# Sigmoid products and convolution diagonals on GpSimd, and another order of the taps on VectorE

## The reference

```python
a = _rmsnorm(h, g_pre_mix[l])
u = jnp.einsum("bsd,dc->bsc", a, w_in[l])            # 1024 -> 2560
c_val, c_gate = u[..., :512], u[..., 512:1024]
qkv = u[..., 1024:].reshape(B, S, 3, 8, 64)
glu = c_val * jax.nn.sigmoid(c_gate)
y = depthwise causal convolution of glu, 31 taps, + conv_b
conv_out = silu(layernorm(y))
attn_out = stick-breaking attention of q, k, v (8 heads), normed per head
y = concat([conv_out, attn_out]) @ w_out[l]
```

## Time and profile before

| | before |
|---|---|
| median of 3 runs | 1856.43 us (1854.65 to 1856.76) |
| the profiled execution | 1856.76 us, span 1855.0 us |
| PE busy | 1810.0 us (98%) |
| DVE busy | 953.5 us (51%) |
| ACT busy | 751.0 us (40%) |
| POOL busy | 104.9 us (6%) |
| mean granted clock of PE | 0.987 |

### The profile page before, as it was taken

How to read it: one execution, slowest core, us unless ns; L and a number is a source line. 1 busy time by engine, 2 the same in 40 slices (tenths; PEclk the granted TensorE clock), 3 DMA queues, 4 the chain that set the end, 5 groups by cost and what they waited for, 6 DMA issues and landing times.

```text
span 1855.0 us, 21601 instructions
## 1 busy us (share of the span) xinstructions
PE 1810.0 (98%) x8477; PEld 1482.7 (80%) x8477; DVE 953.5 (51%) x1714; ACT 751.0 (40%) x1475; POOL 104.9 (6%) x151
## 2 busy tenths in 40 slices
PE   8999999999999999999999999999998999999997
PEld 7887888888887777777888888787887788888886
DVE  6666444344334667655344434487984544243345
ACT  7333432323234556645232323333855543233233
POOL 0000010101001111001010101000000000000000
PEclk9999999999999999999999999999997999999999
DMA  7222233333333112112333332232100332333331
GB/s 250 79 70 90 70 113 91 102 91 102 91 102 84 57 46 69 35 57 80 95 99 96 97 98 95 80 93 78 58 1 1 99 106 92 102 91 102 96 97 57
DMA packets 195749, 158.37 MB, mean 85 GB/s; under 512 B 5249, under 2 KB 161153, under 8 KB 195649
## 3 DMA queue, kind: packets, MB, share of 16 engines
q1 hardware_dynamic: 194240, 154.16, 27.0%
q0 software_dynamic: 400, 1.25, 0.3%
q10 hardware_dynamic: 1008, 1.59, 0.2%
HBM read 154.88 MB, written 2.10 MB: 85 GB/s over the span
## 4 chain that ended last, share of the span: by engine, by line
PE 90%; DVE 6%; ACT 3%; issue 1%; DMA 0%; SPq 0%; ACTq 0%; DVEq 0%
PE ps L730 29%; PE ps L731 28%; PE ps L732 28%; PE ps L1158 1%; PE ps L782 1%; DVE sb L1864 0%; DVE sb L1838 0%; PE ps L1046 0%; DVE sb L2394 0%; ACT sb L1379 0%; PE ps L1052 0%; DVE sb L1836 0%; PE ps L841 0%; DMA sb<-in_mem 0%; PE ps L1022 0%
## 5 line engine op out<-in xcount | busy, mean ns | idle before, releaser
L730 PE MATMUL ps<-sb,sb 128*128 128x512 f32 (+3 forms) x2547 | 987.5, 390 | 6.5 <-issue 2.4
L731 PE MATMUL ps<-sb,sb 128*128 128x512 f32 (+3 forms) x2547 | 965.6, 381 | 0.0
L732 PE MATMUL ps<-sb,sb 128*128 128x512 f32 (+3 forms) x2547 | 965.5, 381 | 0.0
L730 PEld LDWEIGHTS ps<-sb,sb 128*128 128x128 f32 (+1 forms) x2547 | 478.3, 189 | 114.2 <-issue 16.2
L732 PEld LDWEIGHTS ps<-sb,sb 128*128 128x128 f32 (+1 forms) x2547 | 478.0, 189 | 92.0
L731 PEld LDWEIGHTS ps<-sb,sb 128*128 128x128 f32 (+1 forms) x2547 | 478.9, 189 | 85.3
L1838 DVE TENSOR_TENSOR sb<-sb,sb 128x512 fp32r<-128x512 f32 x532 | 348.3, 695 | 348.7 <-ACT sb L1360 347.8
L1360 ACT ACTIVATE sb<-sb 128x512 fp32r<-128x512 f32 x532 | 305.8, 622 | 436.5 <-PE ps L732 434.3
L2053 DVE TENSOR_TENSOR sb<-sb,sb 128x512 fp32r<-128x512 f32 x64 | 68.0, 1063 | 177.0 <-ACT sb L1509 177.0
L1519 ACT ACTIVATE sb<-ps 128x512 f32<-128x512 f32 x64 | 38.4, 599 | 208.6 <-PE ps L732 208.6
L658 POOL TENSOR_TENSOR sb<-sb 128x512 f32<-128x512 f32 x64 | 66.9, 1045 | 785.6 <-ACT sb L1519 785.6
(11 more groups left out here) (203 smaller groups left out, 1001.1 us busy)
## 6 DMA issues: line engine op xcount, KB each, us to landing
sb<-in_w_up SPq DMA_DIRECT2D x86, 512.0 KB, 3.9
sb<-in_w_down SPq DMA_DIRECT2D x86, 512.0 KB, 3.9
sb<-in_w_gate SPq DMA_DIRECT2D x22, 512.0 KB, 3.8
sb<-in_a_w_in SPq DMA_DIRECT2D x20, 512.0 KB, 3.7
sb<-in_w_in SPq DMA_DIRECT2D x20, 512.0 KB, 3.6
sb<-in_w_o SPq DMA_DIRECT2D x16, 512.0 KB, 3.9
sb<-in_w_mem_kv SPq DMA_DIRECT2D x8, 512.0 KB, 7.7
sb<-in_w_out SPq DMA_DIRECT2D x8, 512.0 KB, 3.9
```

What stands on the lines that cost most here:

```text
L730: mm(ps, lh, rh, start=start, stop=False, **k)
L731: mm(ps, lh, rl, start=False, stop=False, **k)
L732: return mm(ps, ll, rh, start=False, stop=stop, **k)
```

## The change

The product of the sigmoid with `RB` and the products that make the diagonals go from DVE's queue to POOL's, in the order of the plan, with the same semaphores. The step `dg` goes. In the plan, the taps stand in other numbers and places: ahead of the attention units 5 for each tile behind the first two and 4 for each `v2` slab (66 in all up to `v2_out`, where 45 were, and three behind it), then two behind each `lg`, two more ahead of `bt`, and two at a unit's end. `lo` stands right behind `ev`, `sl` right behind `sp` and `lo`, and `v2_out` behind the last taps of the `v2` slabs.

```diff
--- before.py
+++ after.py
@@ -379,16 +379,10 @@
     TAPS = [(j, k) for j in range(3) for k in range(31)]
     PLAN_C = []
     for n, x in enumerate(IN_FIRST):
-        PLAN_C += [("tile", x), ("w", SL["in", x] + 3), ("ev", x)]
-        if n < 2:
-            PLAN_C += [("lo", x)]
-        else:
-            PLAN_C += [("taps", 2), ("lo", x), ("taps", 1 if x[0] in "qk" else 2)]
+        PLAN_C += [("tile", x), ("w", SL["in", x] + 3), ("ev", x), ("lo", x), ("taps", 5 if n >= 2 else 0)]
     for j in range(4):
-        PLAN_C += [("v2", j), ("w", CH["v2"].first + min(j, 2) + 3)]
-        if j == 3:
-            PLAN_C += [("v2_out",)]
-        PLAN_C += [("taps", 3)]
+        PLAN_C += [("v2", j), ("w", CH["v2"].first + min(j, 2) + 3), ("taps", 4)]
+    PLAN_C += [("v2_out",)]
     BEHIND = [("tile", x) for x in IN_LATER] + [("cv", g) for g in range(3)] + [("ln_sub",)]
     for u in range(8):
         b = BEHIND[u - 1] if u else ("", "")
@@ -399,8 +393,7 @@
         PLAN_C += [("lg", u), ("taps", 2)]
         if u >= 4:
             PLAN_C += [("pt" if u % 2 else "ps", u // 2 - 2)]
-        if BEHIND[u][0] == "cv":
-            PLAN_C += [("dg", u - 4)]
+        PLAN_C += [("taps", 2)]
         if u >= 1:
             PLAN_C += [("bt", u - 1)]
         if u >= 2:
@@ -412,7 +405,7 @@
             PLAN_C += [("lo", b[1])]
         if u >= 4 and u % 2 == 0:
             PLAN_C += [("pr", u // 2 - 2)]
-        PLAN_C += [("taps", 2), ("sl", u)]
+        PLAN_C += [("sl", u)]
         if u >= 1:
             PLAN_C += [("ah", u - 1), ("at", u - 1)]
         if u >= 2:
@@ -422,7 +415,7 @@
             PLAN_C += [("w", CH["v2"].last + min(u, 3) + 4)]
         if u >= 4 and u % 2:
             PLAN_C += [("pl", u // 2 - 2)]
-        PLAN_C += [("taps", 1 if u < 4 else 4 if u < 6 else 100)]
+        PLAN_C += [("taps", 2 if u < 6 else 100)]
     PLAN_C += [("bt", 7), ("ps", 2), ("va", 6), ("ex", 7), ("pr", 2), ("o", (0, 1, 2)), ("ah", 7), ("at", 7), ("kp", 6),
                ("ln_var",), ("pt", 2), ("ln_rs",), ("va", 7), ("kp", 7), ("pl", 2), ("ps", 3), ("pr", 3), ("ln_mul",),
                ("o", (3,)), ("pt", 3), ("silu", 0), ("pl", 3)]
@@ -705,6 +698,28 @@
                     q.wait_ge(S("sub_hi"), g + 1)
                     TTT(lo[:, :], OT[:, :], hi[:, :].bitcast(F32), ALU.subtract).then_inc(S("sub_lo"), 1)
         mlp(1)
+
+        for step in PLAN_C:
+            if step[0] == "tile" and step[1][0] == "g":
+                j = GATES.index(step[1])
+                q.wait_ge(S("sig"), j + 1)
+                TTT(T4[:, j % 2, :], T4[:, j % 2, :], RB[:, :], ALU.mult).then_inc(S("sig_r"), 1)
+            elif step[0] == "cv":
+
+                taps = CV_GROUPS[step[1]]
+                for part in ([k for k in taps if k < 16], [k for k in taps if k >= 16]):
+                    if not part:
+                        continue
+                    n, k0 = len(part), part[0] % 16
+                    q.wait_ge(S("w_used"), SL["in", "k3"] + 1)
+                    q.wait_ge(S("cw"), 2)
+                    if part[0] >= 16:
+                        q.wait_ge(S("cv_used"), 1 + (part[-1] >= 26))
+                    eye = IDENT.unsqueeze(1).broadcast_to([128, n, 128])
+                    at = slice(part[0], part[-1] + 1)
+                    for dst, w in ((DH, CWH[:, at].bitcast(F32)), (DL, CWL[:, at])):
+                        TTT(dst[:, k0:k0 + n, :], eye, w.unsqueeze(2).broadcast_to([128, n, 128]), ALU.mult).then_inc(
+                            S("diag"), 1)
 
         q.wait_ge(S("values"), 8)
         q.wait_ge(S("mix_lo"), 4)
@@ -2261,8 +2276,6 @@
                 tt(T4[:, j % 2, :], ps, RB[:, :], ALU.mult).then_inc(S("in_ev"), 1)
             elif x[0] == "v":
                 j = GATES.index("g" + x[1])
-                q.wait_ge(S("sig"), j + 1)
-                tt(T4[:, j % 2, :], T4[:, j % 2, :], RB[:, :], ALU.mult).then_inc(S("sig_r"), 1)
                 q.wait_ge(S("sig_r"), j + 1)
                 q.wait_ge(S("edge"), 2)
                 tt(GL[:, int(x[1]), 30:30 + T], ps, T4[:, j % 2, :], ALU.mult).then_inc(S("glu"), 1)
@@ -2272,28 +2285,9 @@
                 stt(QKS[:, i % 2, :], ps, 0.125 if x[0] == "q" else 1.0, RB[:, :], ALU.mult, ALU.mult).then_inc(
                     S("in_ev"), 1)
 
-        def diagonals(g):
-
-            taps = CV_GROUPS[g]
-            for part in ([k for k in taps if k < 16], [k for k in taps if k >= 16]):
-                if not part:
-                    continue
-                n, k0 = len(part), part[0] % 16
-                q.wait_ge(S("w_used"), SL["in", "k3"] + 1)
-                q.wait_ge(S("cw"), 2)
-                if part[0] >= 16:
-                    q.wait_ge(S("cv_used"), 1 + (part[-1] >= 26))
-                eye = IDENT.unsqueeze(1).broadcast_to([128, n, 128])
-                at = slice(part[0], part[-1] + 1)
-                for dst, w in ((DH, CWH[:, at].bitcast(F32)), (DL, CWL[:, at])):
-                    tt(dst[:, k0:k0 + n, :], eye, w.unsqueeze(2).broadcast_to([128, n, 128]), ALU.mult).then_inc(
-                        S("diag"), 1)
-
         def block_step(kind, *a):
             if kind == "w":
                 weights(a[0])
-            elif kind == "dg":
-                diagonals(a[0])
             elif kind == "ev":
                 tile_out(a[0])
             elif kind == "taps":
```

## The result

The changed kernel takes 1867.99 us (median of 6 runs, 1865.89 to 1868.72), the kernel before in the same comparison 1855.54. The ratio, which rests on more executions than these six (15 of the changed kernel), is 1.0075, 95% interval 1.0063 to 1.0086. It is slower by 12.4 us between the medians, where the sum of the prediction had 11.1. The profiled execution took 1870.3 us, with a span of 1868.5.

The account below looks back on a forecast made before the run. TensorE, busy in 98% of the span, was taken as the bound. Lateness of 8.9 us at q2, 8.6 at k3 and 11.1 at the first convolution group was carried to the end: 1856.76 + 11.1 = 1867.9, so 1868, range 1861 to 1875.

Parts of the forecast that it names:

- DVE's queue overfills: Up to `v2_out`: 21 more taps, 15.8 us, against 10.7 us of idle; TensorE 8.9 us late at tile q2.
- The lost cover: Low part right behind the evacuation: VectorE waits 0.77 us for ScalarE's copy, five times, 3.85 us.
- Contention by the sigmoid products: GpSimd's sigmoid products delay VectorE's taps by 1.15 us each, 3.45 us for three gates, against 2.2 saved.
- k3 8.6 us late: Attention units 1 to 3: TensorE stays the bound, so tile k3 starts 8.6 us late, at 1339.7.
- Part 4: Diagonals on GpSimd block VectorE; first convolution group waits for k3's evacuation until 1359.8 instead of 1348.72, 11.1 us late.
- The clock: Granted clock over the whole kernel: no term in the sum, 3 us either way in the range.
- No contention: Rival: GpSimd and VectorE run side by side, q2 5.5 us late, 1862 us; chance 0.20 (1860.5 to 1865).
- POOL much dearer: Rival: diagonal products at twice the estimate cost 9.5 us more, up to 1877; chance 0.17, shared with a lagging clock.
- Absorbed: Rival: VectorE's backlog stays under the 4 us in hand, giving 1856 to 1858 us; chance 0.09.
- faster: Rival: early backlog costs nothing and 1336.7 to 1391.3 returns to clock 1.00, gaining 7 us, 1850 us; chance 0.06.

Follow-up runs that it names:

- e6: Changed kernel with the old numbers of taps ahead of the attention units (48 instead of 66), everything else as changed; 1861.3 us.
- e5: Changed kernel with two of the five taps again between a tile's evacuation and its low part, three behind it; 1863.6 us.
- e10: Changed kernel with every sigmoid product made twice on GpSimd, the first into scratch that nothing reads; 1870.9 us.
- e1: Kernel before with the new order of steps only, sigmoid products and diagonals staying on VectorE; 1861.7 us.
- e11: Changed kernel with the four taps between tile k3's weight halves and the statistic of unit 0's pair put behind that statistic; 1861.4 us.
- e2: Kernel before with its old order of steps, only the sigmoid products and diagonals moved to GpSimd; 1859.7 us.
- e8: Changed kernel with GpSimd's diagonals started when unit 0's pair statistic is out, not when tile k3 is used; 1865.3 us.
- e3: Changed kernel with the sigmoid products on VectorE again, the diagonals still on GpSimd; 1868.5 us.

## Why the prediction was right, and where it wasn't

The number was right (1868 for 1867.99, range 1861 to 1875), and so was the main mechanism, a VectorE queue that overfills ahead of `v2_out`. That the number came out so closely is luck: at logits 5 the kernel is 14.3 us late where 11.1 were forecast for the first convolution group, and 3.1 us came back behind it by a clock that the prediction had left out of its sum.

- **DVE's queue overfills: right.** 82.6 us were worked out and 82.8 measured, and e6 shows that the counts of taps alone decide whether q2 is late. PE's waits are where they were put (k1 and the first three slabs), 1.1 to 1.3 us each for 1.3 to 1.6, and 2.5 at q2 for about 3. q2 is 9.0 late for 8.9.
- **The lost cover: right, a little larger.** 3.85 us were expected, e5 shows 4.6.
- **Contention by the sigmoid products: right in kind, 1.15 each was too much.** The taps of g1 and g2 show 0.92, e10 0.98. The sum of the other terms was 0.9 us too small (e1: 82.3 for 81.3), most of it the cover, which made up for it.
- **k3 8.6 us late: wrong, 11.2.** I let the clock out of the sum. The wait at q2 was followed by 5.6 us at a granted clock of 0.50, in which the first 13 of the 24 products of tile q2 were made; that is the 2 us between 9.0 and 11.1. In e1, where that stretch is half as long (0.50 from 1300.17 to 1303.10), 8.5 becomes 9.4.
- **Part 4, what PE waits for at unit 4: wrong in the event, and its closeness is luck.** The prediction let the first convolution group wait for the evacuation of k3. What PE met first was the statistic of the first pair, for which `values(2)` waits; it stands two more taps behind in DVE's queue. In the step list it was there to be read, and I had followed the queue only up to the evacuation. The length of the chain was wrong as well: from the start of POOL's diagonals to the end of k3's evacuation 14.4 us were worked out, as if the two engines took turns throughout, and it took 8.1 (1350.48 to 1358.60). That is in time: without the wait for the statistic PE would have come to the group at about 1359.5 (an estimate: 1357.54, where the wait begins, and the 1.96 us that `values(2)` takes in e11). So by the mechanism of the prediction this term would have been nothing. The statistic made it 3.2 us for 2.5. What was right is that POOL's four products (8.84 us for 9.5) block DVE's work there, at a cost of 5.9 us in all.
- **The clock: underrated.** From logits 5 on the kernel got 3.1 us back, as the slow piece of the kernel before in units 5 and 6 didn't occur. Without that the result would have been 14 us. The 3 us that I set aside were as large as the largest single shift (2.1 at q2, 3.1 here); that the shifts nearly cancelled wasn't foreseen.
- **The rivals.** No contention: falls (e10, and the 5.55 us in e2). POOL much dearer: falls, it was cheaper. Absorbed and faster (its 7 us are the 54.6 us at clock 0.87 of the earlier trace rows): fall; the queue did overfill, and PE had nothing to gain from a lighter DVE in units 5 to 7, where it is busy without a wait up to logits 7 while DVE idles for up to 7.3 us at a time.

Open: what makes the granted clock fall in one place and not in another. e8 and e11 are alike up to logits 5 but for 1.1 us, and differ by 4.6 us from there to logits 7.

## What to carry to other kernels

When one engine is full, sum the other engines' queues between two events that the full one waits for, not over the span: VectorE was half idle overall and still overfilled in one stretch, so that TensorE was 9 us late behind it, and that set most of the time. Follow such a queue to every step that the full engine waits for, small ones too: a statistic of 0.16 us, queued behind blocked taps, held TensorE for 3.3 us. And work moved to GpSimd wasn't off VectorE here: a sigmoid product on GpSimd cost VectorE 0.98 us (e10), the first four diagonal products together 5.9 us. It mattered more where it landed than how much it was.

## What the runs showed of the hardware that was not expected

- The GpSimd products with broadcast operands were cheaper than the estimate from plain ones: two of 1408 columns took 5.04 us beside a nearly idle VectorE, 1.8 ns for a column, where the rows of before gave 2.14 for each further column, and one of 512 columns took 1.04 us, where a plain one takes 1.27 or more. That the broadcast is the reason isn't shown.
- Blocking is not one for one. Beside 8.84 us of GpSimd products VectorE lost 5.9 us on its weight halves and taps, and an evacuation from PSUM in the middle of them lost nothing (0.68 us). GpSimd's own products were stretched as well: a sigmoid product took 1.86 us among taps, and 1.30 at 1211.80, where it began in a pause of VectorE. So neither engine simply stands for as long as the other works, as the prediction had reckoned.
- In the changed kernel a wait of 2.5 us on TensorE was followed by 5.6 us at a granted clock of 0.50 (the products that start from 1302.97 to 1308.26 are slow); behind four waits of 1.1 to 1.3 us ahead of it, each 7 us apart, it stayed 1.00. The same wait of 2.5 us was followed by less in e1, e3 and e5: over the 7 us behind it the granted clock is 0.76 to 0.79 there and 0.58 in the changed kernel. And the clock can fall without a wait: from logits 4 to logits 5 of the kernel before TensorE is busy for all of the 19.10 us, and the clock is 0.82.
